# Static experts' rows from positions alone, the last tile's router on x2, and fourteen homes for half matrices

## What is computed

```python
    x = x + g1 * jnp.einsum('nte,ed->ntd', mixed, w_out)
    h2 = rmsnorm(x, norm2_g) * (1 + sc2) + sh2
    x = x + g2 * hier_moe(h2, router_g_w, router_g_b, router_e_w, router_e_b, w_gate, w_up, w_down)
...
def hier_moe(h, rg_w, rg_b, re_w, re_b, w_gate, w_up, w_down):
...
    g_prob = jax.nn.softmax((t @ rg_w + rg_b).astype(F32), axis=-1)
    g_star = jnp.argmax(g_prob, axis=-1)
    p_star = jnp.max(g_prob, axis=-1)
    g_hot = jax.nn.one_hot(g_star, N_EXPERT_GROUPS, dtype=F32)
    e_logits = (jnp.einsum('td,gde->tge', t, re_w) + re_b).astype(F32)
    e_sel = jnp.sum(e_logits * g_hot[:, :, None], axis=1)
    top_v, top_i = lax.top_k(e_sel, EXPERT_TOP_K)
    top_w = jax.nn.softmax(top_v, axis=-1) * p_star[:, None]
...
    for g in range(N_EXPERT_GROUPS):
        a = (jax.nn.silu(jnp.einsum('td,edf->tef', t, w_gate[g]))
             * jnp.einsum('td,edf->tef', t, w_up[g]))
        out = out + jnp.einsum('tef,efd->td', a * gw[:, g, :, None], w_down[g])
```

## Time and profile before

| | us |
|---|---|
| median of 3 runs | 829.48 (827.67 to 833.77) |
| the profiled execution, run | 830.8 |
| the profiled execution, span from the first to the last instruction | 828.6 |
| mean granted TensorE clock, share of full speed | 0.906 |
| PE busy (matmuls) / weight loads | 672.9 / 391.4 |
| DVE / ACT / POOL busy | 289.5 / 176.2 / 126.4 |
| bytes moved, mean rate | 211.86 MB, 256 GB/s |

### The profile page before, as it was taken

The page is one execution under the profiler, slowest core; times in us unless marked ns, Lnnn a source line. Parts: engine busy times, 40 slices in busy tenths (PEclk is TensorE's granted clock), DMA queues, the critical chain, the costliest instruction groups (busy, mean ns, idle before and its releaser), DMA issues.

```text
span 828.6 us, 11931 instructions
## 1 busy us (share of the span) xinstructions
PE 672.9 (81%) x4846; PEld 391.4 (47%) x4846; DVE 289.5 (35%) x691; ACT 176.2 (21%) x362; POOL 126.4 (15%) x224
## 2 busy tenths in 40 slices
PE   4668999999998875999994289876899999979800
PEld 3568787888862441434554244323344444323300
DVE  4799747741110542416634611100010011100047
ACT  6010421222232563422111001100110101100033
POOL 2310007559100331200000100000000000000040
PEclk9789999999999987999985589989899999999955
DMA  8995166656858979884219268999998549999562
GB/s 293 379 271 195 57 244 219 206 182 189 206 112 317 365 171 306 335 311 157 78 36 323 94 203 300 339 391 409 396 363 298 209 130 389 396 399 400 215 240 108
DMA packets 93580, 211.86 MB, mean 256 GB/s; under 512 B 8700, under 2 KB 15372, under 8 KB 93237
## 3 DMA queue, kind: packets, MB, share of 16 engines
q1 hardware_dynamic: 82550, 182.48, 62.3%
q0 software_dynamic: 4976, 18.37, 7.6%
q10 hardware_dynamic: 6000, 10.25, 3.4%
HBM read 197.42 MB, written 18.91 MB: 261 GB/s over the span
## 4 chain that ended last, share of the span: by engine, by line
PE 64%; DMA 14%; SPq 9%; DVE 6%; ACT 3%; issue 2%; POOL 1%; ACTq 0%; POOLq 0%; DVEq 0%
PE ps L2458 15%; PE ps L2053 11%; PE ps L2498 9%; PE ps L2364 7%; SPq L644 6%; DMA whalf<-in_w_down 5%; PE ps L1955 4%; DMA ring<-in_cache_v 4%; PE ps L2023 3%; PE ps L1961 3%; SPq L503 2%; DMA ring<-in_ada_w 2%; PE ps L2195 2%; PE ps L2170 1%; DMA ada_half<-in_ada_w 1%
## 5 line engine op out<-in xcount | busy, mean ns | idle before, releaser
L2458 PE MATMUL ps<-whalf,xgT 128*128 128x512 f32 (+2 forms) x576 | 175.1, 624 | 15.7 <-DMA whalf<-in_w_up 11.4
L2458 PEld LDWEIGHTS ps<-whalf,xgT 128*128 128x128 f32 (+2 forms) x576 | 67.5, 159 | 115.6 <-issue 110.7
L2498 PE MATMUL ps<-whalf,aT 128*128 128x512 f32 (+2 forms) x288 | 87.6, 625 | 13.8 <-DMA whalf<-in_w_down 11.9
L2053 PE MATMUL ps<-hT,ring 128*128 128x272 f32 x384 | 91.4, 394 | 0.0
L2053 PEld LDWEIGHTS ps<-hT,ring 128*128 128x128 f32 x384 | 71.8, 190 | 15.2 <-issue 1.4
L2498 PEld LDWEIGHTS ps<-whalf,aT 128*128 128x128 f32 (+2 forms) x288 | 33.3, 159 | 61.1 <-issue 58.7
L2364 PE MATMUL ps<-ring,mixT 128*128 128x512 f32 x128 | 60.0, 627 | 1.9 <-ACT mixT L819 1.9
L789 POOL DMA_INDIRECT xg<-h_d,gidx x12 | 11.5, 954 | 244.1 <-PE ps L1955 210.8
L2023 PE MATMUL ps<-hT,ring 128*32 128x136 f32 x1024 | 36.4, 301 | 5.4 <-DVE hT L1355 4.0
L1842 DVE COPY ysb<-ps 128x512 f32<-128x512 f32 x12 | 8.3, 691 | 92.3 <-PE ps L2498 92.3
L2364 PEld LDWEIGHTS ps<-ring,mixT 128*128 128x128 f32 x128 | 25.2, 201 | 32.2 <-issue 30.0
(11 more groups left out here) (396 smaller groups left out, 913.2 us busy)
## 6 DMA issues: line engine op xcount, KB each, us to landing
whalf<-in_w_down SPq DMA_DIRECT2D x32, 1024.0 KB, 16.1
whalf<-in_w_gate SPq DMA_DIRECT2D x32, 1024.0 KB, 10.2
whalf<-in_w_up SPq DMA_DIRECT2D x32, 1024.0 KB, 14.7
ada_half<-in_ada_w SPq DMA_DIRECT2D x16, 1024.0 KB, 5.4
ring<-in_cache_k SPq DMA_DIRECT2D x8, 1792.0 KB, 7.4
ring<-in_cache_v SPq DMA_DIRECT2D x6, 2048.0 KB, 13.1
ring<-in_ada_w SPq DMA_DIRECT2D x4, 2048.0 KB, 14.6
ring<-in_w_in SPq DMA_DIRECT2D x4, 2048.0 KB, 13.2
```

Of the source, the lines that this page charges most:

```text
L2053: ins = mm(ps[:, z % 2, 0:2 * NCOL], r[:, 512 * k + P * (c % 4):512 * k + P * (c % 4 + 1)], hT[:, k, 2 * h:2 * h + 2, :].rearrange("p a b ...
L2458: ins = mm(out[cols, :], xgT[b][:, k, cols], r[:, 512 * (k % 4):512 * (k % 4 + 1)], start=k == 0, stop=k == KD - 1, **tile_at(m_, n))
L2498: ins = mm(ps[cols, 6 + n2, :], aT[:, t % 2, c, cols], r[:, c0:c0 + 512], start=c == 0, stop=c == 3, **tile_at(m_, n))
```

## The change

It has four parts.

1. **Static rows from positions alone.** A token of a static expert sits in the row that its position gives, without any ranking. So right behind the position matmuls VectorE compares `iotaneg` with the positions in PSUM (`row1h`, two instructions), PE multiplies ten one-hot blocks with `rowtok` (20 matmul instructions), and VectorE copies `gidx` for tiles 0 and 1 only. The rest of the ranking follows as before; the index matmuls of all tiles (`rows_of_tiles`) stand on PE between the gate and the up product of tile 0, and the rest of `gidx` is copied late (`gidx` reaches 2). VectorE's copy of tile 0's transposed rows, `rows(0, 0)`, moves ahead of `slot1h`, and the softmax weights move behind the expert numbers.
2. **The last tile's router on x2.** The last tile of `ORDER3` transposes `x2` itself; its logits use router columns scaled by `1 + sc2` (`rwm`), are multiplied by the token's inverse root in `last_logits`, and get the logits of the shift added (`shift_logits`, `shift_rows`). `h2` of that tile is still made, for the gather, but no longer stands ahead of the logits' matmuls.
3. **The prompt's shift and scale turned on the chip.** SP loads sixteen rows of `mod_d`, PE transposes them (during the attention steps), VectorE copies them to `mod2T`; part 2 needs them with channels on partitions.
4. **Fourteen homes.** `W_SLOTS` is 14. The two new homes lie over routing buffers and old modulation rows, so halves 12 and 13 wait until `gidx` is 2. Group and expert maxima are also found together: `first_max` runs twice over 5 sets of 4 instead of three times over one.

```diff
-W_SLOTS = 12
+W_SLOTS = 14
+STATIC_HALVES = 6 * STATIC
...
+            if i == 1:
+                for b in range(2):
+                    sp.wait_ge(s_modst[b], 64)
+                for c in range(4):
+                    sp.dma_start(mod2r[4 * c:4 * c + 4, :],
+                                 bass.AP(mod_d.tensor, (6 + c) * P * P, [[32 * P, 4], [1, P]])).then_inc(s("cld"), 16)
...
-            if n < W_SLOTS:
+            if n < STATIC_HALVES:
                 continue
...
+            if n < W_SLOTS:
+                sp.wait_ge(s("gidx"), 2)
...
+            if t == STATIC:
+                pool.wait_ge(s("gidx"), 2)
...
+            if st == 8:
+                dve.wait_ge(s("pe_prep"), M2P)
+                v.tensor_copy(mod2T[:, :], ps[:, 7, 0:16]).then_inc(s("dve_prep"), 1)
...
+            o(stt(out=lg[:, j, :], in0=ps[:, 4, 0:20], scalar=stat[:, 56 + j:57 + j], in1=shrows[:, :],
+                  op0=ALU.mult, op1=ALU.add))
...
+                o(tt_(rwm[:, :, :], rw[:, :, :], mod2T[:, 8:16].unsqueeze(2).broadcast_to([P, KD, 20]), ALU.mult))
...
+        first_max(hot1, lg, top1)
+        o(stt(out=flat(lg2), in0=flat(hot1), scalar=NEG, in1=flat(lg), op0=ALU.mult, op1=ALU.add))
+        first_max(hot2, lg2, top2)
...
+        for e in range(STATIC):
+            ins = stt(out=row1h[:, e, :, :], in0=cst("iotaneg").unsqueeze(1).broadcast_to([P, NT, P]), scalar=-1.0,
+                      in1=place[:, :, e:e + 1].broadcast_to([P, NT, P]), op0=ALU.mult, op1=ALU.is_equal)
+        ins.then_inc(s("rM"), 1)
...
+        v.tensor_copy(gidx[:, 0:STATIC], ps[:, 3, 0:STATIC]).then_inc(s("gidx"), 1)
...
+        rows(0, 0)
         tt_(slot1h[:, :, :, :], cst("iotaneg").unsqueeze(1).unsqueeze(1).broadcast_to([P, 2, NT, P]),
...
+        v.tensor_copy(gidx[:, STATIC:NTILE], ps[:, 7, STATIC:NTILE]).then_inc(s("gidx"), 1)
...
+            if st == 6:
+                pe.wait_ge(s("cld"), 80)
+                tr(ps[:, 7, 0:16], mod2r[:, :]).then_inc(s("pe_prep"), 1)
...
+        shift_logits()
+        x2_t()
+        shift_rows()
         logits(NT - 2)
-        h2_t(NT - 1)
-        logits(NT - 1)
+        last_logits()
...
+        for e in range(STATIC):
             for j in range(NT):
-                ins = mm(ps[:, 2, 0:NTILE], slot1h[:, k, j, :], tt[:, k, j, :], start=k + j == 0,
-                         stop=(k, j) == (1, NT - 1))
+                ins = mm(ps[:, 3, e:e + 1], row1h[:, e, j, :], rowtok[:, j, e:e + 1], start=j == 0, stop=j == NT - 1)
...
         gate_in(0)
+        rows_of_tiles()
         up_in(0)
```

More of the change, by code:

```diff
@@ L248, in _build @@
     ering = [at(f"ering{i}", [P, SLOT], RING + 16384 * i) for i in range(R2)]
[L249 removed]
+    whalf = [at(f"whalf{i}", [P, SLOT // 2], off)
+             for i, off in enumerate([RING + 8192 * n for n in range(12)] + [HT + 8192, TAB + 4096])]
     NCC = CONST.shape[1]
@@ L636, in _ @@
                 expert[m] = sp.value_load(ranki[0:1, m - STATIC:m - STATIC + 1], min_val=0, max_val=NE - 1)
[L638 to L641, removed]
-            else:
-                sp.wait_ge(done[old_w], tile + 1)
+            if n < W_SLOTS:
+                sp.wait_ge(s("gidx"), 2)
+            else:
+                old_w, old_m, old_half = next(key for key, at_ in W_ORDER.items() if at_ == n - W_SLOTS)
+                use, tile = W_LAST[old_w, old_m, old_half]
+                if old_half == 0:
+                    sp.wait_ge(s("whalf"), use + 1)
+                else:
+                    sp.wait_ge(done[old_w], tile + 1)
             sp.dma_start(half_dst(w, i), half_src(w, expert[m], half)).then_inc(efull[i], 16)
@@ L1735, in _, with rows @@
[L1735 to L1738, removed]
+        last_logits()
+        def rows(t, b):
+            dve.wait_ge(s("xgp"), t + 1)
+            v.tensor_copy(xgT[b][:, 4:8, :], ps[:, 5, :].rearrange("p (a b) -> p a b", a=4)).then_inc(s("xgd"), 1)
+        sets = lambda a: a[:, :, :].rearrange("p j (g e) -> p j g e", e=4)
@@ L2378, in h2_t, with x2_t, shift_logits, shift_rows @@
                 ins.then_inc(s("hTp"), 1)
+        def x2_t():
+            j = ORDER3[-1]
+            pe.wait_ge(s("x2"), NT)
+            pe.wait_ge(s("hTa"), 2 * NT - 1)
+            pe.wait_ge(s("hTd"), 2 * NT - 1)
+            for half in range(2):
+                for c in range(4):
+                    k = 4 * half + c
+                    ins = tr(ps[:, 6 + half, P * c:P * (c + 1)], x2[:, j, P * k:P * (k + 1)])
+                ins.then_inc(s("hTp"), 1)
+        def shift_logits():
+            pe.wait_ge(s("woa"), NT)
+            out = ps[0:1, 0, 0:20]
+            mm(out, cst("ones", 1)[:, 0:1], rb[:, :], start=True, stop=False)
+            for k in range(KD):
+                ins = mm(out, mod2T[:, k:k + 1], rw[:, k, :], start=False, stop=k == KD - 1)
+            ins.then_inc(s("shl"), 1)
+        def shift_rows():
+            pe.wait_ge(s("dve_prep"), SHLE)
+            mm(ps[:, 1, 0:20], cst("ones", 1)[:, 0:P], shrow[:, :], start=True, stop=True).then_inc(s("shl"), 1)
+        def last_logits():
+            j = ORDER3[-1]
+            pe.wait_ge(s("hTa"), 2 * NT)
+            pe.wait_ge(s("hTd"), 2 * NT)
+            for k in range(KD):
+                ins = mm(ps[:, 4, 0:20], h2T[:, k, tok(j)], rwm[:, k, :], start=k == 0, stop=k == KD - 1)
+            ins.then_inc(s("lg"), 1)
         def logits(p):
```

114 lines of the change are left out of this document (69 added, 45 removed).

## The result

| | kernel before | changed kernel |
|---|---|---|
| median, us (lowest to highest of 4 runs) | 828.94 (827.67 to 833.77) | 807.85 (804.03 to 809.11) |
| ratio, 95% interval | | 0.9711 (0.9673 to 0.9749) |
| profiled execution: run / span | 830.8 / 828.6 | 809.1 / 807.2 |

The change takes 21.1 us off; 806 had been forecast, with 799 to 816 around it. A repeat of the changed kernel with six runs gave 0.9732 (0.9684 to 0.9781).

The account below looks back on a forecast made before the run. Bound: the chain from the last tile's norm through routing to tile 0, then PE's waits for weights. -13.2 (start) and -10.2 (homes) make -23.4: 830.8 to 807.4 profiled, median 806, range 799 to 816.

Parts of the forecast that it names:

- Logits: Last tile's router on x2: logits ready at 441.1 instead of 447.2 at full clock, -6.1; bounds -3.9 and -6.1.
- Maxima: Between last logits and the end of `M`: 4.2 us instead of 5.1, -0.9; bounds 0 and -1.2.
- Static index and gather: Static indices 18.3 earlier; tile 0's gather takes 7.0, losing 2.6; first expert product at 465.4, -15.7.
- Slow start: Tile 0's gate product: 1.5 us of slow start, so it takes 8.6 and ends at 474.0.
- The second `gidx`: Half 12 waits for it, issued at 477 instead of 486.66; the stream meets PE's releases again near 500.
- Homes: Experts' weight stream: two more homes shrink PE's waits by 5.1 in each of two stretches, -10.2; bounds 0 and 23.8.
- the rival that homes bring little: Experts' stage: PE's waits come from the stream's pace alone; 816 if homes bring nothing; chance 0.13.
- the one that a wait less also spares slow starts: Experts' stage: PE's waits shrink more, and the first stretch may gain more than 5 us; 801; chance 0.08.
- Sum: Whole kernel: -13.2 from the start and -10.2 from the homes, -23.4; profiled run 807.4, median 806.
- POOL held by VectorE: Rival at the two static gathers: each could wait for a VectorE instruction, sum 2 us higher; 808; chance 0.03.
- At no cost: SP's small loads, PE's transposes, VectorE's copy and `rw` scaling hide in existing waits; uncovered they would cost 0.3 to 2 us.

Follow-up runs that it names:

- the home order: Changed kernel with homes given out in another order, half 12 taking home 0 and half 13 home 1: 810.1 us, 0.9763 of the kernel before.

## Why the prediction was right, step by step

**Logits: mis-sized.** -6.1 was taken, full clock; -3.8 was measured (15.5 to 11.7 on the common scale), the bound for half clock, -3.9. The step that failed is "Before, PE did nothing from 437 to 439 [...]; now it works there. I take full clock". PE did work from 432 to 436 without a pause, but on small matmuls, and the granted clock fell to 0.50 by 436 all the same. In the repeat it fell later, after the transposes (1.07 us instead of 1.94); the logits came 4.8 earlier than before, and `M` stood at 14.8. With the clock held up by extra matmuls `M` stands at 14.5, so the router on `x2` and the maxima gave 6.0 together, not 7.0. One extra matmul of 1.13 us stands in that chain itself, ahead of the sample's logits; what full clock alone would give is not shown.

**Maxima: right.** From the end of the logits to the end of `M` it was 5.1 before and 4.2 after: -0.9, as forecast.

**Static index and gather: right together, in part by luck.** Position matmuls 2.36, as copied from before; the two one-hot instructions 1.55 (1.7 forecast); the twenty matmuls on one column 4.41 (4.48); so the first `gidx` came 2.0 late on the common scale, by the logits' miss. The gather landed 5.32 after its start instead of 7.0 and gave most of that back. VectorE had its copy `rows(0, 0)` at 466.02 after a wait of 0.42: the forecast that it is just free was right. First product at 466.82, which is 465.8 on the axis of the prediction; forecast 465.4. In the repeat the gather took 7.70, and the first product stood at 35.3 instead of 34.0 although `M` had come 1.1 earlier; that the forecast was met within 0.4 is the luck of this execution.

**Slow start: mis-sized.** 1.5 us had been read from the two products of the earlier trace rows; it was 3.0, as the clock came back only during the gate product's second half. The index matmuls cost 2.14 (2.45 forecast). The up product of tile 0 came 12.0 us earlier instead of 13.2, and 10.8 of it were left at the end without the homes.

**The second `gidx`: right.** Half 12 left at 479.43, 478.4 on the axis of the prediction, forecast 477; the home order showed that its wait costs nothing.

**Homes: right in size, as waits only in part.** -10.2 forecast; 10.8 alone, 11.1 on top of the start. Between the traces with 12 and with 14 homes on top of the start it was 6.0 from tile 0's up product to tile 2's `down` and 5.2 from there on, where 5.1 each had been set. The forecast took all of it as PE's waits for weights. Without the start these fell by 9.6 (23.8 to 14.2), on top of it only by 6.2 (22.2 to 16.0, where about 14 had been forecast); there 4.3 more are matmuls that ran slower behind a wait, such as the 5.34 and 5.11 us shown above. So the rival that homes bring little is out, and the one that a wait less also spares slow starts was right in its mechanism: it made up for waits that shrank less than forecast.

**Sum.** -23.4 forecast, -21.9 measured. Up to tile 0's up product 1.2 are missing: 2.3 at the logits and 1.5 at the slow start, against 1.7 from the gather and small pieces. Another 1.2 of the start were lost behind it, and the homes gave 0.9 more than forecast. The sum is as near as it is because misses of both signs partly cancel. The scatter of the stages before made it 1.06 more in the profiled execution.

**POOL held by VectorE: not tested.** VectorE's `cap_prod` had ended when the first static gather started on POOL; beside it ran a sum over `cap_prod`, one input and one output (timelines of POOL and of VectorE):

```profile
458.58 1.02 POOL L807 DMA_INDIRECT xg<-h_d,gidx  x1 [15.59 <-DVE gidx L1804]
...
457.61 0.96 DVE L1806 TENSOR_TENSOR cap_prod<-rank_onehot,const 128x784 f32<-128x784 f32 x1
458.61 0.97 DVE L1808 TENSOR_REDUCE cap<-cap_prod 128x56 f32<-128x784 f32 x1
```

The rule of the Trainium skill, "SBUF — State Buffer", section "SBUF: two separate sides", speaks of a VectorE instruction in a mode that uses two ports, such as a float32 copy within SBUF, and of one with two inputs in SBUF beside a POOL instruction that reads SBUF. The sum is not of the second kind, and nothing here shows that it is of the first; so the 1.02 us neither bear the rule out nor speak against it.

**At no cost: not separated.** The zero lies between 429.9 and 435.1 in the runs with the turned rows and at 431.75 and 434.99 in the two without; a cost below that scatter can't be excluded.

## What to carry to other kernels

Where a stage changes between being held by its buffers and by its stream, an earlier start and more buffers can be separate gains, as here: each moves a different wait, and a 2 by 2 of runs shows it better than an argument from one trace. A stream that started later cost next to nothing here, as releases set its pace afterwards. To compare a stretch before and after, first shift the window by what the change has gained up to there. And where a chain of small matmuls and waits runs ahead of large products, read the granted clock over the chain itself, and cost every matmul in it at the lower level unless the trace shows the higher.

## What was not expected of the hardware

The granted TensorE clock fell although PE was never idle: in the changed kernel, window by window, PE was busy 2.00 of 2 us with 27 small matmuls while the clock went down.

```profile
432.00:434.00 2.00, 2.00 (x17) 1.37 (x16) 1.20 (x1) 0.28 (x1) 0.00 (x0) 1.00 0.16 9
434.00:436.00 2.00, 2.00 (x27) 1.89 (x27) 1.93 (x3) 0.00 (x0) 0.00 (x0) 0.77 0.83 296
436.00:438.00 2.00, 1.35 (x15) 1.23 (x11) 1.06 (x4) 1.33 (x3) 0.00 (x0) 0.50 0.93 323
```

In the kernel with extra matmuls in all waits (fourteen homes) the same column reads 1.00 in the windows from 436 to 448, and the last logits took 1.96 us instead of 3.60:

```profile
436.00:440.00 4.00, 4.00 (x39) 3.15 (x39) 3.34 (x5) 0.07 (x1) 0.56 (x1) 1.00 1.04 389
440.00:444.00 4.00, 4.00 (x10) 1.75 (x10) 3.53 (x15) 0.00 (x0) 0.00 (x0) 1.00 1.01 356
```

And this one core moved 396 GB/s for 80 us (385 to 410 in windows of 5 us) while PE worked from the same memory:

```profile
485.00:565.00 80.00, 66.85 (x303) 28.37 (x301) 8.96 (x13) 6.84 (x12) 3.76 (x4) 0.96 1.04 396
```

The weights' stream did not slow PE's matmuls: products of 16 matmuls took 7.0 to 7.1 us there as elsewhere at full clock.
